# One copy and one addition for both heads in each level of the block inversion of an RWKV recurrence

## What is computed

```python
def rwkv7_scan(r, decay, k, v, a, bb, s0):
    def step(s, inp):
        r_t, w_t, k_t, v_t, a_t, b_t = inp
        sa = jnp.einsum('bhij,bhj->bhi', s, a_t)
        s = s * w_t[:, :, None, :] + sa[..., None] * b_t[:, :, None, :] + v_t[..., None] * k_t[:, :, None, :]
        return s, jnp.einsum('bhij,bhj->bhi', s, r_t)
    xs = tuple(jnp.moveaxis(z, 1, 0) for z in (r, decay, k, v, a, bb))
    s, ys = lax.scan(step, s0, xs)
    return jnp.moveaxis(ys, 0, 1), s
```

## Time and profile before

| what | us |
|---|---|
| median of 3 runs (3249.28 to 3252.21) | 3249.32 |
| the profiled execution | 3251.43 |
| its span, from the first to the last instruction | 3249.2 |
| mean granted TensorE clock, share of full speed | 0.952 |
| TensorE busy | 2901.1 (89%) |
| VectorE busy | 1273.7 (39%) |
| ScalarE busy | 743.4 (23%) |
| GpSimd busy | 822.6 (25%) |

### The profile page before, as it was taken

How to read it: one execution, slowest core, us unless ns; L and a number is a source line. 1 busy time by engine, 2 the same in 40 slices (tenths; PEclk the granted TensorE clock), 3 DMA queues, 4 the chain that set the end, 5 groups by cost and what they waited for, 6 DMA issues and landing times.

```text
span 3249.2 us, 58439 instructions
## 1 busy us (share of the span) xinstructions
PE 2901.1 (89%) x24095; PEld 2741.5 (84%) x24095; DVE 1273.7 (39%) x2462; ACT 743.4 (23%) x1359; POOL 822.6 (25%) x595
## 2 busy tenths in 40 slices
PE   5996768576699899999999999879789999999997
PEld 4996547455479899999999999847689999999996
DVE  5126555556471321212112489965322221111122
ACT  2002132332260411112111220036323121121211
POOL 3121000000006222323223822200262232232345
PEclk9998779898899999999999999989899999999998
DMA  3110000000011111111111211120211111111112
GB/s 115 45 45 30 2 1 3 1 2 2 20 62 50 35 45 46 39 52 43 41 46 41 86 60 45 37 72 2 75 45 33 48 43 41 51 42 45 44 43 70
DMA packets 51849, 133.95 MB, mean 41 GB/s; under 512 B 7128, under 2 KB 22104, under 8 KB 51432
## 3 DMA queue, kind: packets, MB, share of 16 engines
q1 hardware_dynamic: 51688, 131.61, 12.5%
HBM read 119.68 MB, written 11.92 MB: 40 GB/s over the span
## 4 chain that ended last, share of the span: by engine, by line
PE 69%; DVE 3%; ACT 0%; issue 0%; DMA 0%; SPq 0%; POOL 0%; DVEq 0%; POOLq 0%; ACTq 0%
PE PS L315 20%; PE PS L317 20%; PE PS L316 20%; PE PS L1289 3%; PE PS L1261 2%; PE PS L1315 2%; DVE zc L1448 1%; PE PS L1469 1%; PE PS L1237 0%; DVE h_lo L451 0%; DVE x L1783 0%; PE PS L1275 0%; DVE c_s L1392 0%; PE PS L346 0%; DVE h_lo L706 0%
## 5 line engine op out<-in xcount | busy, mean ns | idle before, releaser
L315 PE MATMUL PS<-h_hi,w_hi 128*128 128x384 f32 (+1 forms) x3456 | 1134.6, 328 | 67.4 <-POOL w_lo L407 26.4
L316 PE MATMUL PS<-h_lo,w_hi 128*128 128x384 f32 (+1 forms) x3456 | 1132.3, 328 | 0.0
L317 PE MATMUL PS<-h_hi,w_lo 128*128 128x384 f32 (+1 forms) x3456 | 1132.0, 328 | 0.0
L407 POOL TENSOR_TENSOR w_lo<-w_raw,w_hi 128x1024 fp32r<-128x1024 f32 (+2 forms) x208 | 470.1, 2260 | 1114.3 <-ACT w_hi L385 1114.3
L315 PEld LDWEIGHTS PS<-h_hi,w_hi 128*128 128x128 f32 x3456 | 652.3, 189 | 68.9 <-issue 68.6
L316 PEld LDWEIGHTS PS<-h_lo,w_hi 128*128 128x128 f32 x3456 | 652.3, 189 | 0.3
L317 PEld LDWEIGHTS PS<-h_hi,w_lo 128*128 128x128 f32 x3456 | 652.1, 189 | 0.0
L385 ACT ACTIVATE w_hi<-w_raw 128x1024 fp32r<-128x1024 f32 (+2 forms) x208 | 201.8, 971 | 915.3 <-PE PS L317 915.3
L317 PE MATMUL PS<-hid_hi,w_lo 128*128 128x384 f32 (+1 forms) x1056 | 346.9, 328 | 0.0
L315 PE MATMUL PS<-hid_hi,w_hi 128*128 128x384 f32 (+1 forms) x1056 | 346.7, 328 | 0.0
L316 PE MATMUL PS<-hid_lo,w_hi 128*128 128x384 f32 (+1 forms) x1056 | 346.6, 328 | 0.0
(11 more groups left out here) (259 smaller groups left out, 2881.3 us busy)
## 6 DMA issues: line engine op xcount, KB each, us to landing
w_raw<-in_w_gu SPq DMA_DIRECT2D x88, 512.0 KB, 3.5
w_raw<-in_w_d SPq DMA_DIRECT2D x48, 384.0 KB, 3.1
w_raw<-in_w_e SPq DMA_DIRECT2D x20, 512.0 KB, 3.5
w_raw<-in_w_o SPq DMA_DIRECT2D x20, 512.0 KB, 3.5
x<-in_x SPq DMA_DIRECT2D x4, 1536.0 KB, 8.9
x_home<-x SPq DMA_DIRECT2D x1, 4352.0 KB, 14.0
w_raw<-in_w_oe SPq DMA_DIRECT2D x8, 512.0 KB, 3.5
w_raw<-in_w_d SPq DMA_DIRECT2D x16, 256.0 KB, 2.6
```

Of the source, the lines that this page charges most:

```text
L315: pe.matmul(out, w_h, a_h, start=k == 0, stop=False)
L316: pe.matmul(out, w_h, a_l, start=False, stop=False)
L317: last = pe.matmul(out, w_l, a_h, start=False, stop=k == kn - 1)
L407: pool.tensor_tensor(w_lo[slot][:, 0:kn, :], w_raw[slot][:, 0:kn, :], w_hi[slot][:, 0:kn, :].bitcast(F32), ALU.subtract).then_inc(sm["w_lo ...
```

## The change

Each level handles both heads at once. ScalarE makes one copy of 128x(2x192) from banks 0 and 1, VectorE one addition of 128x(2x384) from banks 2 and 3 (2x192 in the last level). The four semaphores go up five times a wave. TensorE's matmuls and their order stay. The wait for the start values (`x_init`) stays one per head. The first use of `xx` after the levels waits for the one addition of the last level.

```diff
                     for l in range(LEVELS - 1):
-                        for h in range(2):
-                            act.wait_ge(sm["y_done"], 10 * q + (2 * l + h + 1))
-                            act.activation(y_sb[:, h, :, :].rearrange("p b c -> p (b c)"),
-                                           PS[:, h, 0:WAVE * CHUNK], ACT.Copy).then_inc(sm["ysb_ready"], 1)
+                        act.wait_ge(sm["y_done"], 5 * q + l + 1)
+                        act.activation(y_sb[:, :, :, :].rearrange("p h b c -> p h (b c)"),
+                                       PS[:, 0:2, 0:WAVE * CHUNK], ACT.Copy).then_inc(sm["ysb_ready"], 1)
...
                         if l == 0:
                             pe.wait_ge(sm["x_init"], 2 * q + (h + 1))
-                        else:
-                            pe.wait_ge(sm["xadd"], 10 * q + (2 * (l - 1) + h + 1))
+                        elif not h:
+                            pe.wait_ge(sm["xadd"], 5 * q + l)
                         for b in range(WAVE):
                             for r in halves:
                                 last = pe.matmul(PS[r, h, b * CHUNK:(b + 1) * CHUNK], bt_level[r, l, 3 * h + b, :],
                                                  xx[r, h, 0, b, :], start=True, stop=True)
-                        last.then_inc(sm["y_done"], 1)
+                    last.then_inc(sm["y_done"], 1)
                     for h in range(2):
 
-                        pe.wait_ge(sm["ysb_ready"], 10 * q + (2 * l + h + 1))
+                        if not h:
+                            pe.wait_ge(sm["ysb_ready"], 5 * q + l + 1)
...
-                        last.then_inc(sm["xprod_done"], 1)
+                    last.then_inc(sm["xprod_done"], 1)
 
                 pe.wait_ge(sm["akv_ready"], q + 1)
                 for h in range(2):
-                    pe.wait_ge(sm["xadd"], 10 * q + (8 + h + 1))
+                    pe.wait_ge(sm["xadd"], 5 * q + 5)
...
-                    for h in range(2):
-                        dve.wait_ge(sm["xprod_done"], 10 * q + (2 * l + h + 1))
-                        k0 = 0 if l < LEVELS - 2 else 1
-                        dst = xx[:, h, k0:2, :, :].rearrange("p a b c -> p (a b c)")
-                        dve.tensor_tensor(dst, PS[:, 2 + h, k0 * WAVE * CHUNK:2 * WAVE * CHUNK], dst, ALU.add)\
-                           .then_inc(sm["xadd"], 1)
+                    dve.wait_ge(sm["xprod_done"], 5 * q + l + 1)
+                    k0 = 0 if l < LEVELS - 2 else 1
+                    dst = xx[:, :, k0:2, :, :].rearrange("p h a b c -> p h (a b c)")
+                    dve.tensor_tensor(dst, PS[:, 2:4, k0 * WAVE * CHUNK:2 * WAVE * CHUNK], dst, ALU.add)\
+                       .then_inc(sm["xadd"], 1)
```

## The result

The changed kernel takes 3426.7 us (3420.2 to 3429.8, four runs) against 3249.3 before, a ratio of 1.0542 (95% interval 1.0524 to 1.0560): 177 us slower. The sign was forecast, the size was not: 3345 was given, and 3392 as the upper end.

The account below looks back on a forecast made before the run. An order of dependent steps in the recurrence was taken as the bound, no engine being full. Lost overlap of 90 us plus 6 for the clock made 96, giving 3345 us on the median; own range 3330 to 3362, wider 3330 to 3392.

Parts of the forecast that it names:

- The string of steps: Recurrence levels: y, copy, products, addition run one after another for both heads; 7.50 us more a wave, 90.0 for twelve.
- The clock: Recurrence levels: longer TensorE pauses bring four more clock losses of 1.47 us, taken as 6 us.
- Rival A: Levels: TensorE falls to its lower clock and stays; middle level 6.08 us, total 3384 or 3430 us; chance 0.29.
- the nearer part of A: The lower-clock outcomes that the wider range, 3330 to 3392 us, still takes in.
- the stretch of 412 to 416 us: Around L914: TensorE busy 2.23 of 4 us, pauses of about a microsecond, clock still 1.00; cited against Rival A.
- B: ScalarE and VectorE in the levels: fewer fixed instruction costs save 20 us, giving 3230 us; chance 0.02.
- C: Merged copies and additions execute as two halves, 0.66 and 1.12 us; 20 us on top, 3365 us; chance 0.04.
- ScalarE's wait for y: Sign to look for in the levels: this wait stays about the same per copy.

Follow-up runs that it names:

- fill_y: Changed kernel with two unread matmuls a level behind the y products alone; 3352.9 us, 1.0319.
- warm_after: Changed kernel with unread matmuls in both pauses of each level (2 and 4) and in TensorE's pauses outside the levels; 3329.7 us, 1.0235.
- warm_before: Kernel before the change with unread matmuls in TensorE's pauses outside the levels; 3242.5 us, 0.9977.
- fill24: Changed kernel with unread matmuls in each level, 2 behind y and 4 behind the other products; 3360.1 us, 1.0333.
- copy_only: Kernel before the change with only the copies of both heads merged, additions still one per head; 3316.4 us, 1.0196.
- add_only: Kernel before the change with only the additions of both heads merged, copies still one per head; 3327.6 us, 1.0229.
- fine: Kernel before the change with four additions of 128x192 per level for two of 128x384, products ordered by part; 3256.5 us, 1.0018.

## Why the prediction was wrong

**The string of steps held.** The forecast was 4.56, 4.20 three times and 3.13 us for the levels of a wave. At full clock they were 4.64 and three times 4.26 in the first wave, and fill_y, whose first wave keeps the full clock to its end, has 3.16 for the last (y at 372.89, L953 at 376.05). The 0.06 are mainly one handover: from the end of the addition (363.27 + 0.96 = 364.23) to y (364.37) passes 0.14 us and not 0.07. I had taken the handover of head 1, but the lower bound and the upper one both stood there, and the upper one was right. Copy (0.49) and addition (0.96) were sized right. A wave at full clock takes 25.08 us in fill_y from L771 to L778, 7.80 more than 17.28, or 94 us for twelve where the sum gave 90. warm_after against warm_before has 96, and the last fillers of each wave are in it: behind the last addition, which ends at 410.56, L964 starts only at 410.97.

```profile
409.88 1.16 PE L957 MATMUL PS<-ident 128*128 128x128 f32 x8
410.00 0.56 DVE L1177 TENSOR_TENSOR xx<-PS,xx 128x384 f32<-128x384 f32 x1 [2.60 <-PE PS L953]
410.97 0.33 PE L964 MATMUL PS<-tm,xx 64*64 64x64 f32 x4
```

**The step that failed is the term headed "The clock":** "I take four more losses of that size, 6 us". The lost overlap costs 87 to 96 us, so that of the 177 us 81 to 90 are left for the clock. fill24, with nothing but unread work added, gives 67 of them back, fill_y 74. The mistake was to price the clock by how often it fell in the kernel before. Its levels keep TensorE fed nearly all the time (3.85 of 4 us); the new ones all have the same two pauses, 0.58 and 1.15 us of idle, and 27 of 48 steps met the lower clock.

**Rival A was what happened.** Its price for a low level, 6.08 us, against 6.10 and 6.11 measured, was right. "If two levels of each wave run so", 45 us: it was 27 steps of 48, in part only, and 44 us, so that the two sums agree by luck. What its sum left out is the stage after the levels. The dense products behind them start at the lower level too. In the changed kernel's first wave the last copy in the levels starts at 373.85, and L778 at 383.07, 9.22 us later; in warm_after it is 414.94 - 408.49 = 6.45. Twelve waves of the changed kernel sum up to 378.8 us, 75 more than those of warm_after: 44 from the levels, nearly all of the rest from these tails. So the 3384 of A lacked some 30 us. Its other number, 3430 for four levels in each wave, comes close to the measured 3427, but by luck: the levels lost half of what it gives, and the tails and the stages between the waves the rest. The range reached only into "the nearer part of A" and so left out the measured time.

**The evidence that was weighed wrongly** is the stretch of 412 to 416 us. It was taken to speak against A, since one stretch with two pauses had kept 1.00. But the same stage led to the two waves of 18.75 us as well: ahead of the second wave, from 384 to 388 us, TensorE was busy for 2.47 of 4 us at 0.88, and the next 4 us were granted 0.69. I read two waves on one side and ten on the other, for a stage that comes once in a wave, as the sign of an edge, and the levels would now be next to it in every step. fill_y shows how near: two short matmuls a level took most of it away.

The Trainium skill (TensorE: Matmul & The Clock Gate, section "A second HAM failure mode: psum-queue depth-cycling") was named with rival A: by it, idle moments between groups of matmuls make the clock swing between two levels. The trace agrees: the recurrence was granted 0.69, and the seventh wave has steps of 4.27 and of 6.11 us.

**Rivals B and C.** B, the gain by fewer instructions, did not come: VectorE and ScalarE were each busy 10 us less in the whole run, and the wave got longer. C's halves did not show: 957 ns, not 1.12 us.

**One sign was read wrongly.** ScalarE's wait for y was forecast as about the same per copy. It is 3.77 us at full clock and 4.06 on average, where it was 0.92. The prediction's own string says so: in a step of 4.20 us with a copy of 0.49 ScalarE idles for 3.71.

## What to carry to other kernels

Merging the instructions of two interleaved chains removes fixed costs on engines that wait anyway and turns the overlap into a string; count the string first, from rows at full clock. Then ask whether TensorE's new pauses come in every step. If they do, price the whole stage and what follows it at the lower clock too, and give that case a large chance. How large the pauses may be this study does not say: copy_only and add_only opened pauses in every step as well and lost only 19 and 18 us by the clock, the whole change 81 to 90. A few unread matmuls in the pauses are a cheap test of that, and here also a cure: fill_y won back 74 of 177 us with two in each level. It does not make the change a gain: fill_y is still 102 us slower than the kernel before.

## What was not expected of the hardware

Which pause is filled made little difference: four fillers in the one gave 3358 us, two in the other 3353, both together 3360. And the clock can cost as much as a real improvement gives: fine shortened its waves by 6 us in sum and came out 6 us slower, with 0.83 granted in place of 0.88 and 9 us more between the waves. A gain of a few microseconds in a stage like this can be read only from waves or with the clock held.
